# The transposed factor of a triangular inverse: transposes drained by ScalarE in place of a product and its sums

## The chip, the core and the metric

The kernel runs on one core of a Trainium2 chip. TensorE (PE) multiplies and transposes, VectorE (DVE) and ScalarE (ACT) do elementwise work and read PE's results from PSUM, GpSimd (POOL) splits the weights, and SyncE (SP) starts their loads. Each engine works through its own list of instructions in the order written and waits for the others by semaphores. The metric is device time in microseconds for one launch.

## The reference

The reference is one step of a two-layer decoder over a prompt of 1024 tokens and eight single-token samples. Layer 0 mixes tokens with a gated delta rule: projections to keys, queries, values and gates, a short convolution, then for each of 16 value heads a recurrence over chunks. Layer 1 is a diagonal state-space mixer; a SwiGLU layer follows each. What the change touches is the solve inside a chunk:

```
lmat = jnp.where(strict, jnp.einsum('nbhid,nbhjd->nbhij', kb, kc) * decay, 0.0)
sol = lax.linalg.triangular_solve(eye + lmat, rhs, left_side=True, lower=True, unit_diagonal=True)
```

The kernel does it with chunks of 128 tokens and by the inverse of the 128 x 128 unit triangular matrix.

## The kernel before, in words

The mix phase loops over 8 head groups `i` (one key head with its two value heads). In a group, dense steps project six weight tiles (L464), and then four quads `q` follow. A quad is two chunks times two heads, so four 128 x 128 matrices, held side by side in tiles of 512 columns.

The inverse of a quad is built in `levels` (L609). Y starts as the identity plus the mask of the innermost blocks, and TT_ holds its transpose, made once by four transposes (`first_t`, L506) and a ScalarE copy (L722). Then come six levels, each of which doubles the size of the blocks that are inverted. VectorE masks the matrix with the level's pattern into NM (L957). PE forms P = NM x TT_ (L620), which ScalarE copies to PP in two halves (L821), one half for each head. PE then forms PP x Y (PY, L634), which VectorE adds to Y (L1095). TT_ is brought up to date the same way: a third product (L630, called TP here), and two sums by VectorE (L1093). Level 6 has no TP, since its transpose isn't needed.

Each level has two slots in which other work is put, an even one ahead of P and an odd one between P and the products that use PP. The slots, numbered 0 to 11 in a quad, hold the recurrence over the quad before (`chain`: L517, L523, L529, L530, L536), the decays and the masked product for the next quad (L488, L498), transposes of values and keys (L588, L601), the samples' state (L575, L596), the output gate (L476), and pieces of the output projection of the group before (`out_piece`, L548; the first group has none). On ScalarE and VectorE the same slot numbers hold the halves of that work that belong to them, in their own lists: in slot 5 VectorE does the gate's products (L887, L888), and in slot 6 ScalarE waits for them and copies (L712).

The order is written out by hand in these lists. `p.after(engine, name)` makes an engine wait for a step; `use(b, engine, name)` claims PSUM bank b, waits until its former content has been drained, and notes who will drain this one. P and TP of a half share a bank: P in its first 256 columns, TP in the rest. PY has bank 2.

Of the kernel before, what the change touches and what calls it, by code (L numbers as in the profile page):

```python
# [19 lines left out]
ALU = mybir.AluOpType  # L20
AF = mybir.ActivationFunctionType

P = 128
D = 1024
KT = D // P
T = 1024
# [11 lines left out]
QCH = 2  # L38
# [14 lines left out]
def build(nc, dr, plan):  # L53
    ctx = ExitStack()
    with ctx:
        def sb(name, shape, dt=F32, c=ctx):
            return c.enter_context(nc.sbuf_tensor(name, shape, dt))
# [13 lines left out]
        ident = sb("ident", [P, P])  # L71
        gains = sb("gains", [P, 5, KT])
        ps = ctx.enter_context(nc.psum_tensor("ps", [P, 8, 512], F32))
# [235 lines left out]
        NM, PP, TT_, ATT_0, Y_1, VB, ATT_1, KD, EG, DEC_0, DEC_1, Y_0 = (dwork[:, i] for i in range(12))  # L309
# [101 lines left out]
        def f4(a_):  # L411
            return a_.rearrange("p a b -> p (a b)")

        def gate_cols(q):
            return slice(QCH * CH * q, QCH * CH * (q + 1)) if q < NQ else slice(T, N)
# [16 lines left out]
        def mix_pe(p):  # L432
# [4 lines left out]
            def use(b, who, name):  # L437
                if b in held:
                    p.after(*held[b])
                held[b] = (who, name)  # L440
                plan[("bank", p.pfx + name)] = b
                return b
# [166 lines left out]
            def levels(i, q):  # L609
                gq = f"{i}.{q}."  # L610
                Y = YY[q % 2]
                for l in range(1, 7):
                    slot(i, q, 2 * (l - 1))
                    p.after("DVE", gq + f"NM{l}")
                    for h in range(2):
                        p.after(*(("DVE", gq + f"T{l - 1}.{h}") if l > 1 else ("ACT", gq + "T0")))
                        b = use(h, "ACT", gq + f"P{l}.{h}")
                        for c in range(QCH):
                            j = 2 * h + c
                            ins = nc.tensor.matmul(ps[:, b, c * P:(c + 1) * P], NM[:, j], TT_[:, j], start=True, stop=True)  # L620
                        p.go(ins, gq + f"P{l}.{h}")
                    slot(i, q, 2 * (l - 1) + 1)
                    for h in range(2):
                        p.after("ACT", gq + f"P{l}.{h}")
                        p.after("DVE", gq + f"Y{l - 1}")
                        if l < 6:
                            b = use(h, "DVE", gq + f"T{l}.{h}")
                            for c in range(QCH):
                                j = 2 * h + c
                                ins = nc.tensor.matmul(ps[:, b, 256 + c * P:256 + (c + 1) * P], Y[:, j], PP[:, j], start=True, stop=True)  # L630
                            p.go(ins, gq + f"TP{l}.{h}")
                    b = use(2, "DVE", gq + f"Y{l}")
                    for j in range(4):
                        ins = nc.tensor.matmul(ps[:, b, j * P:(j + 1) * P], PP[:, j], Y[:, j], start=True, stop=True)  # L634
                    p.go(ins, gq + f"PY{l}")
# [39 lines left out]
        def mix_act(a):  # L675
            A = nc.scalar
# [26 lines left out]
            def gate_r(g, w):  # L703
                a.after("PE", g + "ones")
                a.do(A.activation(gate_buf(w), ps[:, a.bank(g + "oln"), 0:2 * w].rearrange("p (h n) -> p h n", h=2), AF.Ln, bias=eps_t[:, 0:1], scale=1.0 / P), g + "oln")
                a.go(A.activation(gate_buf(w), gate_buf(w), AF.Exp, scale=-0.5), g + "or")
# [68 lines left out]
            for i in range(HQK):  # L775
                g = f"{i}."
                e = i - 1
                if i:
                    gate_r(f"{e}.{NQ - 2}.", QCH * CH)
                    for k in (1, 2, 5, 6):  # L780
                        chain(e, NQ - 1, k)
                    gate_hi(f"{e}.{NQ - 2}.", gate_cols(NQ - 2), None)
                    state_out(e)
                evac(i, 0)
                if i:
                    gate_r(f"{e}.{NQ - 1}.", QCH * CH)
                evac(i, 1)
                if i:
                    gate_hi(f"{e}.{NQ - 1}.", gate_cols(NQ - 1), None)
                silu(i, 0)  # L790
                evac(i, 2)
                silu(i, 1)
                A.preload_act_table_set(LOGEXP)
                root(i, 0)
                decay(i, 0)
                evac(i, 3)
                root(i, 1)
                silu(i, 2)
                silu(i, 3)
                A.dma_start(dr["cso"][i], cso[:, :, :, :]).then_inc(out_conv, 16)  # L800
                A.dma_start(dr["cpo"][i], cpo[:, :, :]).then_inc(out_conv, 16)
                if i + 1 < HQK:
                    A.dma_start(cst[:, :, :, :], dr["cin"][i + 1]).then_inc(in_conv, 16)
                if i:
                    a.after("DVE", f"{e}.{NQ - 1}.og")
                for t in range(2):
                    for n in range(NC3):
                        a.after("PE", g + f"c{4 + t}.{n}")
                        a.go(A.activation(zb[:, t, blk(n)], ps[:, a.bank(g + f"z{t}.{n}"), 0:NB], AF.Silu), g + f"z{t}.{n}")
                        if t == 1 and n == 1:  # L810
                            first_t(i, 0)
                A.preload_act_table_set(LOGEXP)
                for q in range(NQ):
                    gq = f"{i}.{q}."
                    for l in range(1, 7):
                        slot(i, q, 2 * (l - 1))
                        for h in range(2):
                            a.after("PE", gq + f"P{l}.{h}")
                            if l > 1:
                                a.after("PE", gq + f"PY{l - 1}")  # L820
                            a.go(A.activation(f4(PP[:, 2 * h:2 * h + 2]), ps[:, h, 0:256], AF.Copy), gq + f"P{l}.{h}")  # L821
                        slot(i, q, 2 * (l - 1) + 1)
                    if q + 1 < NQ:
                        first_t(i, q + 1)
# [15 lines left out]
        def mix_dve(v):  # L840
            V = nc.vector
# [62 lines left out]
            def pairs(ap):  # L904
                return ap.rearrange("p (c n) -> p c n", n=P)
# [144 lines left out]
            for i in range(HQK):  # L1050
                g = f"{i}."
                e = i - 1
                if i:
                    chain(e, NQ - 1, 0)
                    scale_q(e, NQ - 1)
                    gate_sq(e, NQ - 2)
                    gate_mul(e, NQ - 2)
                    for k in (3, 4, 7):
                        chain(e, NQ - 1, k)
                tables(i)  # L1060
                if i:
                    gate_lo(e, NQ - 2)
                    gate_sq(e, NQ - 1)
                conv(i, 0)
                if i:
                    gate_mul(e, NQ - 1)
                    gate_lo(e, NQ - 1)
                squares(i, 0)
                conv(i, 1)
                squares(i, 1)  # L1070
                conv(i, 2)
                unit_norm(i, 0)
                decay(i, 0)
                conv(i, 3)
                unit_norm(i, 1)
                triangle(i, 0)
                first_y(i, 0)
                level_mask(i, 0, 1)
                for q in range(NQ):
                    gq = f"{i}.{q}."  # L1080
                    Y = YY[q % 2]
                    for l in range(1, 7):
                        slot(i, q, 2 * (l - 1))
                        if l < 6:
                            level_mask(i, q, l + 1)
                        elif q + 1 < NQ:
                            level_mask(i, q + 1, 1)
                        v.after("DVE", gq + f"Y{l - 1}")
                        for h in range(2):
                            hh = slice(2 * h, 2 * h + 2)  # L1090
                            if l < 6:
                                v.after("PE", gq + f"TP{l}.{h}")
                                v.go(V.tensor_tensor(TT_[:, hh], pairs(ps[:, h, 256:512]), TT_[:, hh], ALU.add), gq + f"T{l}.{h}")  # L1093
                        v.after("PE", gq + f"PY{l}")
                        v.go(V.tensor_tensor(Y, ps[:, 2, :].rearrange("p (j n) -> p j n", n=P), Y, ALU.add), gq + f"Y{l}")  # L1095
                        slot(i, q, 2 * (l - 1) + 1)
# [897 lines left out]
```

## Time and profile before

| | us |
|---|---|
| median of 3 runs | 3890.07 (3887.57 to 3891.27) |
| the profiled execution's own time | 3887.29 |
| its span | 3885.5 |
| PE busy in it | 3545.1 (91%) |
| VectorE busy | 2123.1 (55%) |
| ScalarE busy | 845.5 (22%) |

Busy time is summed over the instructions of an engine. PE stands for the matrix work and PEld for the loads of the stationary operand, which overlap it. The granted clock is the share of TensorE's full clock, 1.00 for 2.4 GHz and 0.50 for 1.2 GHz, as a mean over the stretch. The whole execution has 0.959. A program's fp32 product shows as two matrix instructions.

### The profile page before, as it was taken

The numbers are of one execution on the slowest core, as the hardware profiler recorded it, in microseconds if no ns is written. First come the engines' busy times: TensorE is split into PE (matmuls) and PEld (weight loads), VectorE is DVE, ScalarE is ACT, GpSimd is POOL, SyncE is SP. The second block draws the span as 40 slices with busy tenths as digits, with TensorE's granted clock in tenths as the row PEclk, the third lists the DMA queues.
The fourth block names the chain that finished last, engine by engine and source line by source line (L and its number), as shares of the span: only waits on it lengthen the run. The fifth ranks groups of instructions, "written<-read, shape, count | busy, mean of one in ns | idle before, by whom it ended". The sixth has DMA issues, their size and how long they took to land.

```text
span 3885.5 us, 56613 instructions
## 1 busy us (share of the span) xinstructions
PE 3545.1 (91%) x23849; PEld 3439.2 (89%) x23849; DVE 2123.1 (55%) x4331; ACT 845.5 (22%) x1691; POOL 836.9 (22%) x773
## 2 busy tenths in 40 slices
PE   4999999999999999997889999997679699999997
PEld 3989999998989898996879999996569699999997
DVE  3576757566666767575477577554632333333424
ACT  2333232423333332323100110111210210000001
POOL 1202020201111020201223232322323133323331
PEclk7999999999999999999989999999779899999998
DMA  2101010101001010100112222223831011111111
GB/s 78 34 23 36 28 41 17 41 23 40 29 30 40 23 36 28 35 17 29 33 40 75 71 70 77 71 77 110 231 90 49 22 44 49 44 50 49 45 49 55
DMA packets 91965, 197.29 MB, mean 51 GB/s; under 512 B 23232, under 2 KB 51008, under 8 KB 90560
## 3 DMA queue, kind: packets, MB, share of 16 engines
q1 hardware_dynamic: 65344, 152.42, 12.1%
q10 hardware_dynamic: 26368, 41.25, 3.2%
q8 instruction: 189, 3.10, 0.3%
q14 instruction: 64, 0.52, 0.0%
HBM read 152.69 MB, written 40.94 MB: 50 GB/s over the span
## 4 chain that ended last, share of the span: by engine, by line
PE 78%; DVE 17%; issue 2%; ACT 2%; DMA 1%; SPq 1%; POOL 0%; ACTq 0%; DVEq 0%; POOLq 0%
PE ps L210 25%; PE ps L464 14%; PE ps L1162 11%; PE ps L634 4%; PE ps L548 4%; PE ps L630 4%; PE ps L620 3%; PE ps L240 2%; PE ps L488 1%; DVE dwork L1095 1%; PE ps L523 1%; PE ps L536 1%; DVE hlo L269 1%; DVE S L987 1%; PE ps L476 1%
## 5 line engine op out<-in xcount | busy, mean ns | idle before, releaser
L210 PE MATMUL ps<-hhi,whi 128*128 128x344 f32 x2520 | 811.5, 322 | 87.2 <-DVE hlo L269 72.2
L210 PE MATMUL ps<-hhi,wlo 128*128 128x344 f32 x2520 | 808.8, 321 | 0.0
L210 PE MATMUL ps<-hlo,whi 128*128 128x344 f32 x2520 | 807.9, 321 | 0.0
L1843 POOL TENSOR_TENSOR wtick<-wtick 128x1 f32<-128x1 f32 x213 | 43.0, 202 | 2846.8 <-PE ps L210 977.6
L210 PEld LDWEIGHTS ps<-hhi,whi 128*128 128x128 f32 x2520 | 477.4, 189 | 90.5 <-issue 66.2
L1846 POOL TENSOR_TENSOR wlo<-wraw,whi 128x1024 fp32r<-128x1024 f32 x213 | 527.5, 2477 | 17.1
L210 PEld LDWEIGHTS ps<-hhi,wlo 128*128 128x128 f32 x2520 | 476.8, 189 | 0.0
L210 PEld LDWEIGHTS ps<-hlo,whi 128*128 128x128 f32 x2520 | 476.5, 189 | 0.0
L1215 DVE TENSOR_TENSOR ab<-ps,sg 128x344 f32<-128x344 f32 x132 | 68.2, 516 | 639.5 <-PE ps L210 628.1
L464 PE MATMUL ps<-hhi,whi 128*128 128x344 f32 x1152 | 386.2, 335 | 4.4 <-DVE dwork L847 1.9
L1162 PE MATMUL ps<-ahi,whi 128*128 128x344 f32 x1056 | 342.7, 325 | 32.3 <-DVE ab L1215 29.9
L464 PE MATMUL ps<-hhi,wlo 128*128 128x344 f32 x1152 | 371.7, 323 | 0.0
L464 PE MATMUL ps<-hlo,whi 128*128 128x344 f32 x1152 | 370.8, 322 | 0.0
L1162 PE MATMUL ps<-ahi,wlo 128*128 128x344 f32 x1056 | 340.8, 323 | 0.0
L1162 PE MATMUL ps<-alo,whi 128*128 128x344 f32 x1056 | 340.2, 322 | 0.0
L1230 DVE TENSOR_TENSOR x<-ps,x 128x344 f32<-128x344 f32 x528 | 257.8, 511 | 149.8 <-PE ps L1162 149.8
L1162 PEld LDWEIGHTS ps<-ahi,whi 128*128 128x128 f32 x1056 | 200.8, 190 | 37.9 <-DVE ab L1215 33.3
L464 PEld LDWEIGHTS ps<-hhi,whi 128*128 128x128 f32 x1152 | 219.5, 191 | 9.6 <-issue 8.8
L821 ACT ACTIVATE dwork<-ps 128x256 f32<-128x256 f32 x384 | 144.5, 383 | 362.7 <-PE ps L620 352.1
L464 PEld LDWEIGHTS ps<-hlo,whi 128*128 128x128 f32 x1152 | 219.2, 190 | 4.2 <-issue 3.4
L1844 POOL CAST whi<-wraw 128x1024 fp32r<-128x1024 f32 x213 | 221.5, 1040 | 0.0
L464 PEld LDWEIGHTS ps<-hhi,wlo 128*128 128x128 f32 x1152 | 219.4, 190 | 0.0
(328 smaller groups left out, 6092.2 us busy)
## 6 DMA issues: line engine op xcount, KB each, us to landing
wraw<-in_w SPq DMA_DIRECT2D x213, 512.0 KB, 3.3
tab<-keep_tab SPq DMA_DIRECT2D x8, 1088.0 KB, 6.4
S<-in_sin ACTq DMA_DIRECT2D x16, 512.0 KB, 3.5
out_sout<-S ACTq DMA_DIRECT2D x16, 512.0 KB, 2.6
keep_u<-hs SPq DMA_DIRECT2D x8, 580.0 KB, 3.0
uu<-keep_u SPq DMA_DIRECT2D x8, 580.0 KB, 7.9
keep_tab<-cp ACTq DMA_DIRECT2D x8, 576.0 KB, 6.1
keep_y<-yg SPq DMA_DIRECT2D x64, 68.5 KB, 2.3
```

What stands on the lines that cost most here:

```text
L210: ins = nc.tensor.matmul(out, w, r[:, kt, blk(n)], start=k == 0, stop=k == 3 * KT - 1)
L240: ins = nc.tensor.matmul(ps[:, banks + n, 0:NB], ones[:, :], nsq[:, kt % 2, blk(n)], start=kt == 0, stop=kt == KT - 1)
L464: ins = nc.tensor.matmul(ps[:, b, 0:NB], w, r[:, kt, blk(n)], start=k == 0, stop=k == 3 * KT - 1)
L548: ins = nc.tensor.matmul(ps[:, b, 0:NB], w[:, s, c:c + P], r[:, kt, blk(n)], start=k == 0, stop=k == 5)
L620: ins = nc.tensor.matmul(ps[:, b, c * P:(c + 1) * P], NM[:, j], TT_[:, j], start=True, stop=True)
L630: ins = nc.tensor.matmul(ps[:, b, 256 + c * P:256 + (c + 1) * P], Y[:, j], PP[:, j], start=True, stop=True)
L634: ins = nc.tensor.matmul(ps[:, b, j * P:(j + 1) * P], PP[:, j], Y[:, j], start=True, stop=True)
L821: a.go(A.activation(f4(PP[:, 2 * h:2 * h + 2]), ps[:, h, 0:256], AF.Copy), gq + f"P{l}.{h}")
L1162: ins = nc.tensor.matmul(out, w[:, s, c:c + P], r[:, e % 2, kt, blk(n)], start=q == 0, stop=q == 5)
L1230: v.go(V.tensor_tensor(x[:, m, blk(n)], ps[:, v.bank(f"x{e}.{m}.{n}"), 0:NB], x[:, m, blk(n)], ALU.add), f"x{e}.{m}.{n}")
L1844: G.tensor_copy(whi[:, slot, :], wraw[:, slot, :]).then_inc(w_hi, 1)
L1846: G.tensor_tensor(wlo[:, slot, :], wraw[:, slot, :], whi[:, slot, :].bitcast(F32), ALU.subtract).then_inc(w_split, 1)
```

## The change

TP and its two sums are gone. In their place, at levels 2 to 6 and after the even slot, PE waits for Y of the level before, transposes its four matrices (two for each half, into the columns where TP was), and ScalarE copies each half into TT_. P waits for that copy. ScalarE has the new copies behind what its even slot holds and ahead of the two copies of P.

```
                 for l in range(1, 7):
                     slot(i, q, 2 * (l - 1))
+                    if l > 1:
+                        p.after("DVE", gq + f"Y{l - 1}")
+                        for h in range(2):
+                            b = use(h, "ACT", gq + f"T{l - 1}.{h}")
+                            for c in range(QCH):
+                                ins = nc.tensor.transpose(ps[:, b, 256 + c * P:256 + (c + 1) * P], Y[:, 2 * h + c], ident[:, :])
+                            p.go(ins, gq + f"Tt{l - 1}.{h}")
                     p.after("DVE", gq + f"NM{l}")
                     for h in range(2):
-                        p.after(*(("DVE", gq + f"T{l - 1}.{h}") if l > 1 else ("ACT", gq + "T0")))
+                        p.after("ACT", gq + (f"T{l - 1}.{h}" if l > 1 else "T0"))
                         b = use(h, "ACT", gq + f"P{l}.{h}")
...
                     for h in range(2):
                         p.after("ACT", gq + f"P{l}.{h}")
                         p.after("DVE", gq + f"Y{l - 1}")
-                        if l < 6:
-                            b = use(h, "DVE", gq + f"T{l}.{h}")
-                            for c in range(QCH):
-                                j = 2 * h + c
-                                ins = nc.tensor.matmul(ps[:, b, 256 + c * P:256 + (c + 1) * P], Y[:, j], PP[:, j], start=True, stop=True)
-                            p.go(ins, gq + f"TP{l}.{h}")
                     b = use(2, "DVE", gq + f"Y{l}")
```

On ScalarE:

```
                         slot(i, q, 2 * (l - 1))
+                        if l > 1:
+                            for h in range(2):
+                                a.after("PE", gq + f"Tt{l - 1}.{h}")
+                                a.go(A.activation(f4(TT_[:, 2 * h:2 * h + 2]), ps[:, h, 256:512], AF.Copy), gq + f"T{l - 1}.{h}")
                         for h in range(2):
                             a.after("PE", gq + f"P{l}.{h}")
```

On VectorE:

```
                         v.after("DVE", gq + f"Y{l - 1}")
-                        for h in range(2):
-                            hh = slice(2 * h, 2 * h + 2)
-                            if l < 6:
-                                v.after("PE", gq + f"TP{l}.{h}")
-                                v.go(V.tensor_tensor(TT_[:, hh], pairs(ps[:, h, 256:512]), TT_[:, hh], ALU.add), gq + f"T{l}.{h}")
                         v.after("PE", gq + f"PY{l}")
```

## Rows read from the trace of the kernel before

**Rows 1.** The windows view over the eight groups: us, busy (count) by engine, clock, DMA.

```profile
166.00:1786.00 1620.00, 1536.76 (x11396) 1490.74 (x11395) 1085.64 (x2379) 530.63 (x1136) 211.39 (x171) 0.99 0.09 31
```

**Rows 2.** Waits of PE, 166 to 1785 us: total us, times, longest.

```profile
PE ps L596 <- DVE S L987: 18.9, 7, 2.7
PE ps L523 <- DVE dwork L968: 18.8, 20, 1.5
PE ps L476 <- DVE gsq L881: 16.6, 9, 2.2
PE ps L601 <- DVE S L987: 6.4, 7, 0.9
...
PE ps L529 <- DVE dwork L942: 4.4, 7, 0.6
```

**Rows 3.** Timeline, group 0, quad 3, level 6: start, us, engine, instruction [idle before].

```profile
272.70 0.97 PEld L634 LDWEIGHTS ps<-dwork 128*128 128x128 f32 x8
...
273.59 0.47 PEld L588 LDWEIGHTS ps<-ident,qkv 128*128 128x128 f32 x4
273.70 0.60 PE L588 MATMUL ps<-ident,qkv 128*128 128x128 f32 x4
273.90 0.69 DVE L1095 TENSOR_TENSOR dwork<-ps,dwork 128x512 f32<-128x512 f32 x1 [0.47 <-PE ps L634]
274.03 0.97 PEld L620 LDWEIGHTS ps<-dwork 128*128 128x128 f32 x8
...
274.34 0.60 ACT L763 ACTIVATE dwork<-ps 128x512 f32<-128x512 f32 x1 [1.52 <-PE ps L588]
...
274.83 0.78 ACT L821 ACTIVATE dwork<-ps 128x256 f32<-128x256 f32 x2
274.92 0.25 PEld L601 LDWEIGHTS ps<-ident,qkv 128*128 128x128 f32 x2
275.03 0.38 PE L601 MATMUL ps<-ident,qkv 128*128 128x128 f32 x2
275.73 0.97 PEld L634 LDWEIGHTS ps<-dwork 128*128 128x128 f32 x8 [0.55 <-ACT dwork L821]
```

**Rows 4.** Single lines, their instructions: duration in ns, minimum, median and maximum.

```profile
L630 PE MATMUL ps<-dwork x1280: 270/275/377, 169.1 to 1776.0; 128*128 128x128 f32 x183
...
L588 PE MATMUL ps<-ident,qkv x128: 272/273/273, 187.6 to 1777.4; 128*128 128x128 f32 x128
...
L821 ACT ACTIVATE dwork<-ps x384: 365/384/387, 168.7 to 1778.6; 128x256 f32<-128x256 f32 x192
...
L1093 DVE TENSOR_TENSOR dwork<-ps,dwork x320: 406/424/426, 170.0 to 1776.6; 128x256 f32<-128x256 f32 x160
```

**Rows 5.** Timeline, group 3, quad 1, level 3, whose odd slot is empty.

```profile
835.87 1.02 PEld L620 LDWEIGHTS ps<-dwork 128*128 128x128 f32 x8
...
836.67 0.83 ACT L821 ACTIVATE dwork<-ps 128x256 f32<-128x256 f32 x2 [5.08 <-PE ps L620]
...
837.11 0.97 PEld L630 LDWEIGHTS ps<-dwork 128*128 128x128 f32 x8 [0.22 <-ACT dwork L821]
```

**Rows 6.** Timeline, group 2, quad 3, level 4.

```profile
690.50 0.69 DVE L1095 TENSOR_TENSOR dwork<-ps,dwork 128x512 f32<-128x512 f32 x1 [0.47 <-PE ps L634]
...
691.53 1.02 PEld L620 LDWEIGHTS ps<-dwork 128*128 128x128 f32 x8
...
693.03 0.63 ACT L712 ACTIVATE ohi<-qkv 128x512 fp32r<-128x512 f32 x1 [4.51 <-DVE qkv L888]
...
693.69 0.52 PEld L523 LDWEIGHTS ps<-dwork 128*128 128x128 f32 x4 [1.15 <-DVE dwork L968]
```

**Rows 7.** Windows view: quad 0 of groups 4 and 3, and around one wait of L476.

```profile
1003.90:1037.80 33.90, 31.19 (x259) 30.84 (x258) 24.84 (x57) 8.12 (x17) 3.07 (x2) 1.00 0.05 16
...
789.30:824.60 35.30, 32.59 (x257) 32.36 (x256) 24.81 (x57) 8.06 (x17) 3.03 (x2) 0.95 0.05 16
...
708.00:714.00 6.00, 4.63 (x17) 4.15 (x18) 2.75 (x6) 1.32 (x2) 0.00 (x0) 0.72 0.00 0
```

## The prediction

> **What bounds the kernel now.** I read the windows view first. From 166 to 1786 us, where the eight head groups run (projections and the levels of the triangular inverse), PE is busy 1536.8 of 1620 us at a granted clock of 0.99, VectorE 1085.6 and ScalarE 530.6 [rows 1]. PE is the bound there; the change touches nothing outside it. What PE idles is in the waits view: almost all of it ends on a VectorE instruction of the quads (L968, L987, L881, L942), and the sums of L1093 are not among them [rows 2]. So the question for each edit is what it does to PE's own sequence: work taken out, and new waits put in. VectorE's relief as such is worth nothing.
>
> One level on PE is now: an even slot of filler, P (L620), an odd slot, TP (L630), PY (L634). In the timeline of a level without a wait each of these groups of four products takes 0.89 us of PE's issue time (PY at 272.70, the next group at 273.59) [rows 3]. The two new inputs of the next P, T's halves, are summed by VectorE while PE does PY, so P never waits for them.
>
> **The change, part by part.** There are 5 exchanges in a quad, 4 quads in a group, 8 groups: 160, and 20 in a group.
>
> *The product TP goes, transposes come.* L630 has 1280 records for the 640 products the code issues, so a product is two passes; L588 has 128 for 128 transposes, one pass [rows 4]. Four transposes take 0.44 us (L588 at 273.59, L620 at 274.03) [rows 3]. Saved: 0.89 - 0.44 = 0.45 us each, 9.0 us a group, 72 us in all. The 320 sums of 0.42 us (L1093) leave VectorE and 320 copies of 0.38 us (L821's form) go to ScalarE [rows 4]: neither is the bound, 0 by themselves.
>
> *Wait B, between the transposes and P.* Nothing stands between them in PE's order, so PE waits out a whole drain. Worked from [rows 3]: two transposes (L601) start at 274.92 and leave the array at 275.03 + 0.38 = 275.41, 0.49 later; ScalarE starts 0.04 after the last transpose (L588 ends 274.30, L763 starts 274.34); a half takes 0.38 [rows 4]; from its end to PE's next load 0.06 (L821's first half ends 837.05, L630 loads at 837.11, [rows 5]) to 0.12 (275.61 to 275.73, the end of L821 and the load of L634). Sum 0.97 to 1.03 from the first transpose. PE's queue is free 0.44 after it: B = 0.56 us. The second half follows 0.38 behind the first while P's first half occupies 0.45, no more wait. 18 of the 20 exchanges: 10.1 us.
>
> *The other two* are level 4 of quads 2 and 3. There ScalarE's queue holds, ahead of the T copies, the gate's copy L712, which waits for L887 and L888 on VectorE. Y is done at 690.50 + 0.69 = 691.19, L712 at 693.03 + 0.63 = 693.66 [rows 6]. Now P starts at 691.53 without caring. Then: T's first half at 694.04, P at 694.1, 2.9 after Y; the transposes are off PE's queue 0.79 after Y (filler up to 691.53, then 0.44). Wait 2.13, two a group: 4.3 us. Behind P stands today's wait of L523 for L968 (load at 693.69, P issued by 692.42): 1.25 us, which is over before P is; it is given back, -2.5 a group.
>
> *Wait A, before the transposes.* They need Y, which PE used to need only a P and an odd slot later. Y ends 1.00 after PY is off the queue (273.59; 273.90 + 0.69) [rows 3]; with 0.06 to PE that is 1.06. Filler of the even slots, counted in the code: 0.89 to 0.90 in nine exchanges of a group (an out_piece, or the four products of a chain step or of drow), wait 0.16 each; 0.44 in two (level 6 of quads 1 and 3, the vT transposes), 0.62 each; 1.3 or more in nine, none. 2.7 us, and 0.3 for level 2 of quad 0, where the mask (L957) holds Y back by more than TP used to hide: 3.0 a group.
>
> *PY now waits for both halves of PP.* TP began after the first: PE loads it 1.24 after P (835.87 to 837.11), while the second half ends at 837.50, 1.63 after P [rows 5]. Only where the odd slot is short is it seen: 0.48 in quad 1 level 3, 0.35 in quad 2 level 1, 0.22 in quad 3 level 3. 1.1 us a group.
>
> *Given back elsewhere.* At level 6, kT and the transposes for T0 wait for VectorE (L601 for L987, 6.4 us in 7 times [rows 2], and some 0.6 for L936 in quad 1). P comes 1.0 to 1.6 later after Y5 than now, so both go: 0.9 + 0.6. In quad 3, L529's 0.6 [rows 2] turns into a wait for Y, which comes 0.85 (two sums) sooner: I take 0.4. The long wait of L596 (2.7 us, 7 times) hangs on Y5 and stays. -1.9 a group.
>
> Sum for a group: -9.0 + 10.1 + 4.3 - 2.5 + 3.0 + 1.1 - 1.9 = +5.1 us; seven groups 36 us. The first group has no out_pieces: six even slots lose their 0.9 of cover (5.4) and short odd slots add about 1: 11.5 us. Together +47 us.
>
> *The clock.* The waits of L476 come to 16.6 us in 9 times and those of L596 to 18.9 us in 7 [rows 2]. Where the clock fell, after L596's wait at 818.3, quad 0 of that group took 35.3 us at a mean of 0.95; the same quad of the next group, with the same wait and the clock at 1.00, took 33.9 [rows 7]. A fall to the lower level costs 1.4 us. Read window by window in the same way, it fell behind 6 of the 7 waits of L596, behind 4 of the 8 of L476 (one stands in [rows 7], 0.72 over six us), and behind none of the waits up to 1.5 us that L523 has. The 16 new waits of 2.13 us lie between the two kinds, nearer to L476's, at 0.5 to 0.6: 9 falls, 13 us. Bounds: 0 and 16 x 1.4 = 22 us.
>
> +60 us on the profiled run's own 3887.3 us (its span of 3885.5 and 1.8 around it) is 3947; the median of the runs shown lies 2.8 above it: **3950 us**.
>
> Against this change stands a rule of the Trainium skill, "TensorE: Matmul & The Clock Gate", Part 4 (PE-mode transpose): work in transpose mode does not count as PE being busy the way products do, so it does not hold the full clock. The trace allows it: the four L588 transposes stand right ahead of L596's wait, after which the clock fell more often than after L476's, which has none. By the rule each exchange's 0.44 us adds to the idle time beside it; by row it doesn't. It is the second rival.
>
> **Rivals.**
> 1. *The waits that VectorE causes absorb the new ones.* If P's later start also swallowed what is left of L523's 18.8 us and half of L476's 16.6 us, and B and A came out at their low ends (0.53, 0.10), the sum falls by 2 + 8 + 4 + 9, with no falls of the clock 13 more: 3914. Against: L476 hangs on work after the last level. 10%.
> 2. *The clock goes with the transposes.* Waits A and B and the transposes between them make 0.62 + 0.44 + 0.56 = 1.6 us in level 6 of quads 1 and 3, and 1.06 + 0.44 + 0.56 = 2.1 in six levels of the first group; if those 22 places and all 16 long ones drop the clock, it is 38 x 1.4 = 53 us in place of 13: 3990. For: the share of falls behind L596 against L476. Against: the transposes cut these waits in two, and today's waits up to 1.5 us had none behind them. 13%.
> 3. *Faster: the drain is hidden.* The mechanism is B alone. If P could start while ScalarE drains, as PY does behind PP's drains under an odd slot, 18 x 8 x 0.56 = 81 us go from the 60: 3869. It decides at B = 0.56 - 60/144 = 0.14 us: under that the change gains. A half's copy alone is 0.38, and PE's order holds nothing to put beside it, so 5%.
>
> **How the numbers follow.** Forecast 72%, rivals 10, 13 and 5%. The range, 3912 to 3995, spans rivals 1 and 2 and the bounds of A and B (0.05 us on 160 exchanges is 8 us each way) and leaves the third out. No change that a measurement of this kernel can tell is within 0.2%, 7.8 us: 3%, from a still larger rival 1. Faster 6%, slower 91%.
>
> **What would show it.** L630's records gone and 640 new single-pass ones in their place; PE's idle time in the levels up by 110 to 130 us (A, B and PY's wait, less what is given back), put down to ScalarE copies and L1095's sum, while PE's busy time falls by about 70; P's load 0.97 to 1.03 after the first transpose; a wait of 2.1 us in level 4 of quads 2 and 3, and none of L523's 1.0 there; mean clock of the stretch at 0.97 to 0.98 rather than 0.99. B under 0.3 us, or a level that was bound by VectorE after all (its wait for PY at L1095 gone from the trace), would make the prediction wrong.

## The result and the profile after

The kernel after takes 3932.61 us (median of 4 runs, 3929.4 to 3934.34) against 3888.82 us of the kernel before beside it: a ratio of 1.0114, 95% interval 1.0097 to 1.0132, 44 us slower. Forecast were 3950 us with a range of 3912 to 3995: right in its sign and in its range, 17 us too much in its size.

The profiled execution has 3934.23 us and a span of 3932.5. The eight groups now run from 166 to 1830 us instead of 1785 [rows 1]. What comes behind them takes nearly the same (PE busy 1897 us in the last 2102 us, 1898 in the last 2099 before): 45 of the 47 us between the two spans are lost in the levels. First the windows view of that stretch, then PE's waits in it (total us, times, longest). PE stands for the products, PEld for the loads of the stationary operand, and a PEld wait is what PE's queue stood still for.

```profile
166.00:1830.00 1664.00, 1522.17 (x10755) 1423.02 (x10755) 974.12 (x2059) 637.95 (x1456) 211.39 (x171) 0.98 0.10 30
```

```profile
PEld ps L627 <- ACT dwork L821: 101.4, 160, 1.9
PEld ps L619 <- DVE dwork L1095: 33.0, 77, 1.1
PEld ps L596 <- DVE S L992: 20.6, 7, 2.9
PEld ps L635 <- ACT dwork L826: 18.7, 34, 1.9
...
PEld ps L529 <- DVE dwork L947: 12.0, 7, 1.7
...
PEld ps L523 <- DVE dwork L973: 7.0, 17, 1.2
...
PEld ps L601 <- DVE S L992: 1.1, 7, 0.2
```

In the kernel after, L619 are the transposes, L821 the copies of T, L627 is P, L826 the copies of P, L635 PY. The top row is wait B: P waits for the T copy in all 160 places, 101 us. The second is wait A, the fourth PY's wait. The same view of before, for four rows that the change shortened or lengthened:

```profile
PEld ps L523 <- DVE dwork L968: 26.7, 34, 1.7
...
PEld ps L601 <- DVE S L987: 7.8, 7, 1.1
...
PEld ps L506 <- DVE dwork L936: 6.4, 8, 0.8
...
PEld ps L529 <- DVE dwork L942: 5.8, 7, 0.8
```

L523's and L601's waits shrank as forecast (by 20 and 7 us). L506's, with 2.1 more us in another row, is gone: 8.5 us, where I had 5. L529's doubled where I had it shrink.

The timeline of group 3, quad 1, into level 4 shows one exchange (start, us, engine; a part of the longer rows is another level):

```profile
862.25 0.52 PEld L619 LDWEIGHTS ps<-ident,dwork 128*128 128x128 f32 x4
862.41 0.60 PE L619 MATMUL ps<-ident,dwork 128*128 128x128 f32 x4
862.83 0.66 ACT L821 ACTIVATE dwork<-ps 128x256 f32<-128x256 f32 x2 [2.29 <-PE ps L619]
863.26 0.86 PEld L627 LDWEIGHTS ps<-dwork 128*128 128x128 f32 x7 [0.49 <-ACT dwork L821]
```

P loads 1.01 us after the first transpose. From [rows 3] I had 0.97 to 1.03. Where the transposes themselves begin after a wait it is 0.91: there the first of them starts with its load, while here it starts 0.16 behind it (862.25 and 862.41); I had not made this difference. The other kind of wait, level 4 of quad 3 in the same group:

```profile
928.65 0.69 DVE L1095 TENSOR_TENSOR dwork<-ps,dwork 128x512 f32<-128x512 f32 x1 [1.00 <-PE ps L635]
...
929.70 0.52 PEld L619 LDWEIGHTS ps<-ident,dwork 128*128 128x128 f32 x4
...
931.18 0.63 ACT L713 ACTIVATE ohi<-qkv 128x512 fp32r<-128x512 f32 x1 [3.84 <-DVE qkv L893]
...
931.72 0.64 ACT L821 ACTIVATE dwork<-ps 128x256 f32<-128x256 f32 x2
932.13 0.97 PEld L627 LDWEIGHTS ps<-dwork 128*128 128x128 f32 x8 [1.92 <-ACT dwork L821]
...
933.02 0.53 PEld L523 LDWEIGHTS ps<-dwork 128*128 128x128 f32 x4
```

The gate's copy (L713, L712 of before) stands ahead of T's copies exactly as in [rows 6]; Y is done at 929.34, P loads 2.79 later, and L523 no longer waits. But the clock, which I had fall after such waits, stayed at 1.00 over this one. The windows view, around this wait and around one of L596's waits (the clock is the number before the last two):

```profile
929.00:935.00 6.00, 4.31 (x34) 4.06 (x33) 3.42 (x7) 2.95 (x9) 0.17 (x2) 1.00 0.00 0
1059.00:1065.00 6.00, 3.51 (x15) 3.11 (x16) 2.77 (x8) 1.13 (x3) 0.00 (x0) 0.72 0.00 0
```

I counted the falls of the clock in the stretch of the levels: 11 before, 15 after. Only 1 of the 16 waits of level 4 has one beside it; all 7 of L596's have.

### The profile page after: what moved, and what is told of

It reads as the page before. It is cut to its first block, busy times and chain, and to the rows that moved or that the text cites. A ratio compares the mean times of both kernels' runs of the same rounds, so it can differ in the third digit from the quotient of the medians.

```text
span 3932.5 us, 55272 instructions
## 1 busy us (share of the span) xinstructions
PE 3529.4 (90%) x23209; PEld 3371.0 (86%) x23209; DVE 2012.1 (51%) x4011; ACT 953.2 (24%) x2011; POOL 838.3 (21%) x773
## 4 chain that ended last, share of the span: by engine, by line
PE 76%; DVE 16%; ACT 3%; issue 2%; DMA 2%; SPq 0%; POOL 0%; DVEq 0%; ACTq 0%; POOLq 0%
PE ps L210 24%; PE ps L464 14%; PE ps L1162 11%; PE ps L627 5%; PE ps L635 4%; PE ps L548 4%; PE ps L240 2%; ACT dwork L821 2%; PE ps L488 1%; PE ps L619 1%; DVE dwork L1095 1%; PE ps L596 1%; PE ps L529 1%; PE ps L476 1%; DVE n_r L1371 1%
## 5 line engine op out<-in xcount | busy, mean ns | idle before, releaser
L210 PEld LDWEIGHTS ps<-hhi,whi 128*128 128x128 f32 x2520 | 477.6, 190 | 90.3 <-issue 66.0
L210 PEld LDWEIGHTS ps<-hhi,wlo 128*128 128x128 f32 x2520 | 477.2, 189 | 0.0
L210 PEld LDWEIGHTS ps<-hlo,whi 128*128 128x128 f32 x2520 | 476.7, 189 | 0.0
L464 PE MATMUL ps<-hhi,whi 128*128 128x344 f32 x1152 | 386.1, 335 | 4.4 <-DVE dwork L852 1.9
L464 PE MATMUL ps<-hhi,wlo 128*128 128x344 f32 x1152 | 370.3, 321 | 0.0
L464 PE MATMUL ps<-hlo,whi 128*128 128x344 f32 x1152 | 369.7, 321 | 0.0
L627 PE MATMUL ps<-dwork 128*128 128x128 f32 x1536 | 224.7, 290 | 61.9 <-ACT dwork L821 61.5
L627 PEld LDWEIGHTS ps<-dwork 128*128 128x128 f32 x1536 | 192.4, 195 | 101.4 <-ACT dwork L821 101.4
L1095 DVE TENSOR_TENSOR dwork<-ps,dwork 128x512 f32<-128x512 f32 x192 | 132.6, 691 | 270.5 <-PE ps L635 270.5
L962 DVE TENSOR_TENSOR dwork<-dwork,lev 128x512 f32<-128x512 f32 x192 | 144.5, 753 | 195.6 <-PE ps L627 193.9
L1181 ACT ACTIVATE sg<-ps 128x344 f32<-128x344 f32 x132 | 59.3, 457 | 706.3 <-PE ps L210 706.3
```

What stands on the lines that cost most here:

```text
L210: ins = nc.tensor.matmul(out, w, r[:, kt, blk(n)], start=k == 0, stop=k == 3 * KT - 1)
L464: ins = nc.tensor.matmul(ps[:, b, 0:NB], w, r[:, kt, blk(n)], start=k == 0, stop=k == 3 * KT - 1)
L962: v.go(V.tensor_tensor(NM, DEC[q % 2], lev[:, 1 + l].unsqueeze(1).to_broadcast([P, 4, P]), ALU.mult), g + f"NM{l}")
```

## The experiments

Each is an edit on the kernel before or after, or on an earlier one of them. The first four ran beside the kernel before at 3886.7 us, the next four at 3887.15, the last two at 3890.3.

**e1_bare: the product alone.** On before; TP and its sums taken out, nothing put in. The transpose stays that of level 1.

```
-                        if l < 6:
-                            b = use(h, "DVE", gq + f"T{l}.{h}")
...
-                            p.go(ins, gq + f"TP{l}.{h}")
```

> The kernel before without TP and its two sums, and with nothing in their place; TT_ keeps the transpose that it has at level 1, so the inverse is left incomplete. This prices the product alone. By my terms: 160 x 0.89 = 143 us less, and 9 more because PY then waits for both halves of PP; the waits that VectorE causes stay: 3755 to 3770 us. If instead the levels were held by VectorE's or ScalarE's chain (P, copy, PY, sum), the product would be mostly hidden: 3830 or more.

Measured 3763.75 us, ratio 0.9684 (0.967 to 0.9699), 123 us less. TP was on the path nearly in full. Quad by quad the trace gives 3.97 and 4.1 us less in quads 1 and 2, of 5 x 0.89 = 4.45; and 3.07 in quad 3, where L529's wait grows to the 12 us that the kernel after has too. So this wait is not the transposes' doing: without TP, PE comes to it 0.9 us sooner.

**e2_both: PY's wait alone.** On before.

```
-                    for h in range(2):
-                        p.after("ACT", gq + f"P{l}.{h}")
+                    p.after("ACT", gq + f"P{l}.1")
+                    for h in range(2):
```

> The kernel before, but PE waits for both halves of PP ahead of TP. This prices the term of PY's wait by itself. By my terms it costs 1.05 us in each group and about 1 more in the first: 9 us, 3898. If the wait is covered by the odd slots everywhere: 3889, no change.

Measured 3888.29 us, ratio 1.0009 (1.0 to 1.0018): 3.5 us by the ratio, and by its interval anything from nothing to 7, so under the 9 that I expected. The trace has it. The places are the forecast ones: quad 1 level 3 +0.45, quad 2 level 1 +0.29, quad 3 level 3 +0.15, and 0.16 comes back at the level behind the first. 0.73 us a group instead of 1.05. This trace has 7 falls of the clock in the levels where before has 11, though the edit adds no work: so a difference of four falls between two traces need not come from an edit.

**e3_noB: wait B taken away.** On after; the copies are made, into a tile that nothing reads, and P works on the first transpose.

```
-                        p.after("ACT", gq + (f"T{l - 1}.{h}" if l > 1 else "T0"))
+                        p.after("ACT", gq + "T0")
...
-                            b = use(h, "ACT", gq + f"T{l - 1}.{h}")
+                            b = use(2, "ACT", gq + f"T{l - 1}.1") if h == 0 else 2
...
-                                a.go(A.activation(f4(TT_[:, 2 * h:2 * h + 2]), ps[:, h, 256:512], AF.Copy), gq + f"T{l - 1}.{h}")
+                                a.go(A.activation(tsink[:, :], ps[:, 2, 256 * h:256 * h + 256], AF.Copy), gq + f"T{l - 1}.{h}")
```

> The kernel after, with the same transposes and the same number and width of ScalarE copies, but from PY's bank into a tile that nothing reads (bf16), and with P not waiting for them; P works on the first transpose, so the inverse is left incomplete. This takes wait B alone away. The trace of after shows B at about 0.5 us in 18 places of a group and 2.0 in two, of which some 0.8 comes back as L523's wait: 8 x (18 x 0.5 + 2 x 1.2) = 91 us less, some 5 given back at level 6: 3840 to 3855. The rival, that the loss is the clock (transposes that don't hold it): B gone and the time still near 3920, with as many falls of the clock.

Measured 3839.24 us, ratio 0.9878 (0.9865 to 0.9892): 93 us less than after. Against it, 0.45 to 0.52 us went in the ordinary places (medians over groups 1 to 7) and 1.1 to 1.2 net in each long one: P comes 1.9 sooner there, and some 0.8 returns as L523's wait. The trace has 9 falls of the clock for the 15 of after, which at 1.4 us each is 8 of the 93. This settles the cause of the loss: with the product's 0.45 us saved and B not paid, the kernel is 1.2% under the one before.

**e4_prod and e8_twice: passes, and transposes and the clock.** A pass here is one matrix instruction of the profile. On after; each transpose as a plain product with the identity, and each transpose done twice in transpose mode.

```
-                                ins = nc.tensor.transpose(ps[:, b, 256 + c * P:256 + (c + 1) * P], Y[:, 2 * h + c], ident[:, :])
+                                ins = nc.tensor.matmul(ps[:, b, 256 + c * P:256 + (c + 1) * P], Y[:, 2 * h + c], ident[:, :], start=True, stop=True)
```

```
+                                for _ in range(2):
+                                    ins = nc.tensor.transpose(ps[:, b, 256 + c * P:256 + (c + 1) * P], Y[:, 2 * h + c], ident[:, :])
```

> The kernel after, with each transpose done as a plain product with the identity, which gives the same numbers. If a plain product is two passes and a transpose one, PE works 160 x 0.45 = 72 us more, of which the wait for the first half's copy hides about 0.2 us each: +35 to +50, 3970 to 3985. By the Trainium skill's rule that transposes don't count as PE being busy, the clock should fall less often than the 15 times of the kernel after and some of it comes back, 10 us at most. If the passes don't matter: 3933.

> The kernel after, with each of the 640 transposes issued twice into the same columns. PE's order and the time of each group are those of e4_prod (two passes for each), only in transpose mode. So 0.27 us more for an exchange where nothing else waits, 39 us by my terms: 3970, less what the clock does. e4_prod came to 3955 with 5 falls of the clock in these stages against 15 of the kernel after. If transposes hold the clock as products do: 3955 and few falls. By the Trainium skill's rule that they don't: 15 falls or more, and 3965 to 3975.

Measured 3954.93 us (ratio 1.018, 1.0165 to 1.0196) and 3952.15 us (1.0169, 1.0155 to 1.0183): +22 and +20 us over after (26 and 21 by the ratios). The first is under my 35 to 50; the second is near the 3955 us that I gave it if transposes hold the clock as products do. The two are alike in PE's work, as their traces say:

```profile
L619 PEld LDWEIGHTS ps<-ident,dwork x1280: 186/192/333, 170.2 to 1843.0; 128*128 128x128 f32 x183
```

```profile
L620 PEld LDWEIGHTS ps<-ident,dwork x1280: 137/140/230, 170.5 to 1842.3; 128*128 128x128 f32 x183
```

The first is e4_prod, 1280 records for 640 products, the second e8_twice, 1280 for 1280 transposes; after has 640. So the step's saving rests on passes, one against two. An exchange costs 0.27 us more in e4_prod and 0.22 in e8_twice, not 0.45, since wait B shrinks (PEld waits for the T copy some 54 and 62 us, in after 101). That makes 35 to 43 us; the traces have 6 and 8 falls of the clock where after has 15 (I had first stopped counting at 1830 us, ahead of e4_prod's sixth at 1849), which would give some of it back at 1.4 us each (13 and 10 us). The Trainium skill's rule ("TensorE: Matmul & The Clock Gate", Part 4) is not borne out here: 640 more passes in transpose mode went with fewer falls, not more, and with the time of the products. Five of after's falls stand beside no wait of L476 or L596; of these e4_prod and e8_twice have only the first, at 170 us. But before and e2_both differ by four falls as well, and that twice the work fills PE and so holds the clock would fit both; one trace of each can't show it.

**e5_gate: the long waits.** On after.

```
-                if s == 6 and q >= 2:
+                if s == 7 and q >= 2:
                     gate_hi(f"{i}.{q - 2}.", gate_cols(q - 2), f"{i - 1}.out{KT - 1}.{q - 2}" if i else None)
```

> The kernel after, with ScalarE's copy of the gate (L713 of after) in slot 7, behind the copies of T and P of level 4, instead of slot 6 ahead of them. If the 2.0 us waits of level 4 in quads 2 and 3 are this copy's doing, they go down to 0.5, and L523 waits some 0.25 for VectorE: 16 x 1.25 = 20 us less, 3913. If they came from VectorE's own queue (the gate's products), nothing changes: 3933. If VectorE then stands at the gate's subtraction, it is slower than 3933.

Measured 3910.37 us, ratio 1.0065 (1.0047 to 1.0083): 22 us less than after (19 by the ratios), level 4 of quads 2 and 3 shorter by 1.18 each, and nothing else moved in the other quads. PE's longest wait for a T copy falls from 1.7 us to 0.3:

```profile
PE ps L627 <- ACT dwork L821: 61.5, 151, 1.7
```

```profile
PE ps L627 <- ACT dwork L821: 38.5, 151, 0.3
```

(The first is after, the second e5_gate.) One copy, placed where it cost nothing before, was nearly half of the loss. With the long waits gone the trace still has 14 falls of the clock for the 15 of after, so hardly any of them came from those waits.

**e6_split and e7_both: work behind the transposes.** On after; each slot can be called in parts, and the part that ScalarE doesn't drain comes between the transposes and P. e7_both has e5_gate's edit too.

```
+                        slot(i, q, 2 * l - 3, 1)
+                        slot(i, q, 2 * (l - 1), 1)
                     p.after("DVE", gq + f"NM{l}")
...
+                    slot(i, q, 2 * (l - 1), 2)
                     slot(i, q, 2 * (l - 1) + 1)
...
+                late = s in (6, 9)
+                if q and s in CHAIN_SLOT and part == late:
...
+                if piece and i and part == (s in (3, 7, 9) or s == 2 and q > 0):
```

> The kernel after, with work that ScalarE doesn't drain put between the transposes and P: the out_pieces of slots 3, 7 and 9 and of slot 2, the gate's sums, the chain's kS of slot 6 and its last product of slot 9; and the second drow of quad 0 behind P of level 6. Nothing is left out. By my terms wait B goes in about 15 of 20 places, 0.3 to 0.5 us each, some 2 us at level 6 of quad 0 where P passes L596's wait, and PY's wait takes 0.8 back in quad 3: 8 to 9 us a group, 60 to 67 us, 3866 to 3873, faster than the kernel before. If the waits only move (Y or PP late instead): 3915 or more.

> e6_split and e5_gate in one. Of the 20 us of e5_gate 15 are left, since the chain's kS already covers part of it and L523's wait for L968's sums grows to about 0.65: 3852 to 3858. The rival, that VectorE is the bound once PE's waits are gone: no gain over e6_split.

Measured 3878.68 us (ratio 0.9981, 0.9972 to 0.999) and 3854.48 us (0.9914, 0.99 to 0.9928). Both are faster than the kernel before, and e7_both is where I expected it. e6_split gained 52 us on after by the ratios, 8 short of its 60 to 67: quads 0 to 2 are 5.1, 2.2 and 1.7 us shorter than in after, but quad 3 is 1.05 longer. The timeline of e7_both in group 3, quad 3, level 5 has the reason (POOL is GpSimd; L966 is the mask, L1099 Y's sum, L620 the transposes):

```profile
901.40 2.38 POOL L1850 TENSOR_TENSOR wlo<-wraw,whi 128x1024 fp32r<-128x1024 f32 x1
...
901.59 2.73 DVE L966 TENSOR_TENSOR dwork<-dwork,lev 128x512 f32<-128x512 f32 x1
...
904.25 0.68 DVE L1099 TENSOR_TENSOR dwork<-ps,dwork 128x512 f32<-128x512 f32 x1
904.98 0.42 PEld L620 LDWEIGHTS ps<-ident,dwork 128*128 128x128 f32 x4 [2.10 <-DVE dwork L1099]
```

The mask takes 2.73 us instead of 0.69 while GpSimd subtracts; the sum of Y stands behind it, and now the transposes wait for Y. The moved out_piece is the last reader of its weights and starts that split.

Part of the gain in quad 0 is not wait B at all: L596's wait, 20.6 us in both before and after, is gone from the list, since the second drow now stands behind P of level 6.

**e9_keep7 and e10_late0: where the split falls.** On e7_both, then on e9_keep7.

```
-                if piece and i and part == (s in (3, 7, 9) or s == 2 and q > 0):
+                if piece and i and part == (s in (3, 9) or s == 7 and q < 3 or s == 2 and q > 0):
```

```
-        PIECE_SLOTS = (... (0, 3, 4, 6, 7), (0, 3, 4, 6, 7))
+        PIECE_SLOTS = (... (0, 3, 4, 6, 7), (1, 3, 4, 6, 7))
```

> e7_both, but in quad 3 the out_piece of slot 7 stays in its odd slot. In e7_both that piece is the last to use its weights and sits ahead of P of level 5; GpSimd starts to split the next weights behind it, and VectorE's mask for level 6 (L966) takes 2.7 us instead of 0.7 at its side, which makes Y and with it the transposes 2 us late. If that is the cause, the mask is back at 0.7, and of the 2 us a group some 0.5 is given back as wait B and PY's wait is 0.4 better: 7 x 2 = 12 to 15 us less than e7_both's 3854, 3840. If L966's length has nothing to do with the piece: 3854 to 3858.

> e9_keep7, and the first out_piece of quad 3, after which the other weights' half is free, moved from slot 0 to slot 1. L529's wait of 1.5 us in each of 7 groups stands behind a gate product (L942 of before) that takes 2.57 us beside GpSimd's split. By the same cause the split now starts some 1.5 us later, on instructions of VectorE that nobody waits for at once: up to 7 x 1.5 = 10 us less, 3830. If it then falls on the mask of level 3 or the scaling of keys, the wait only moves: 3840 or a few us more.

e9_keep7: 3859.63 us, ratio 0.9917 (0.9904 to 0.9931), no better than e7_both's 0.9914. Its trace has the mask of quad 3 at its normal length, PE's waits for Y at 26.9 us in place of 36.5 and quad 3 0.84 us shorter. But its profiled run is 3844.86 us while the other five lie at 3858 to 3862; their mean granted clock is 0.955 to 0.958 against 0.962. Of the runs of before beside e7_both, the two at 0.957 took 3891.5 and 3892.9 us and the two at 0.962 3879.5 and 3887.2, so the clock may well be most of the 15 us. The mechanism is seen in a trace, worth 6 us in seven groups where I had 12 to 15, and the gain is not measured. e10_late0: 3838.67 us, ratio 0.9868 (0.9854 to 0.9882), 19 us less than e9_keep7 by the ratios. But the two profiled runs are only 5.4 us apart (3844.86 and 3839.47), so how much of the 19 is the edit and how much e9_keep7's clock isn't shown. What the trace shows is near the 10 that I gave it: L529's wait is gone from its list, PE's wait at L523 grows from 7.8 to 15.1 us, and quad 3, from one quad's end to the next, is 1.6 us shorter, 11 us in seven groups; the row of e9_keep7 that went (L951 is L942 of before):

```profile
PE ps L529 <- DVE dwork L951: 10.6, 7, 1.5
```

It is the fastest of the kernels that build the whole inverse, 1.3% under the kernel before, with the transposes in it. Whether it is the transposes that win is not shown: no run gives the kernel before the same order. Two of the moves need no transposes, and the waits that they take away, 20.6 us at L596 and 5.8 at L529, are in before too: together as much as half of the 51 us.

## Why the prediction was right, and where it was not

*The sum.* By quad, in groups 1 to 7 (median of P of level 1 to PY of level 6, after less before) the trace has +1.8, +1.1, +0.1 and +2.0: 4.9 us a group against 5.1 forecast, and +14.2 in the first group against 11.5. That is 48.5 us for the quads, but it holds six more falls of the clock than before, some 8 us at 1.4 each: about 40 us without the clock where I had 47. Between the groups there are two falls less (-3), and so the stretch grew by 45.

*The saving, 0.45 us.* Right: two passes against one (e4_prod, e8_twice), and TP wholly on the path (e1_bare).

*Wait B.* 101 us measured as PE's queue saw it, 115 forecast (8 x 14.4), the term of the sum that was most too large. e3_noB gives 93 us for it net of what comes back. 0.49 in most of the ordinary places for my 0.56, 1.9 in the long ones for my 2.13.

*Waits A and PY's.* 33 us for A against 29 (8 x 3.0 and the first group's bare slots, 5.4); PY's wait 18.7 us where PE already waited 7.7 for PP before (L630 and L634), 11 more for my 9 to 10. By itself it is less, 0.73 a group (e2_both).

*Given back.* L523 -20 us and L601 -7 as forecast, L506 -8.5 for my 5. L536's 2.9 us went too, which I had not counted. The 0.4 at L529 was wrong: TP's going brings PE to it sooner and it costs 6 us more instead, which e1_bare shows without any transposes.

*The clock, +13 us.* This is the step that failed. I put the new 2 us waits between L476's and L596's by their length and gave them 9 falls; 1 of 16 had one, and e5_gate, without these waits, has 14 falls for 15. I had also compared unlike measures: my 2.13 was a stand of PE's queue, and by that measure L476's waits are 2.16 and L596's 2.94, so the new ones did not lie between the two. The count went from 11 to 15, 6 us at 1.4 each: three new ones in the first group, where bare slots bring waits A and B together, two in level 3 of quad 0, where PE has only its 0.5 us waits, one more at L596, and two fewer at L476 and at a wait of L464 between the groups. What sets the long waits of level 4 apart from L476's, which have falls at nearly the same length, I don't know: PE's own idle time beside them is 1.7 us against 1.97, and the work around them is as dense.

*The 17 us.* The profiled runs lie 46.9 us apart (3934.2 and 3887.3) and I had 60: 13 us too much, of which the clock term is 7 and the rest of the sum 6. I then added 2.8 us for the median of before over its profiled run; after has its median 1.6 under it.

*The readout of PE's busy column* was also off. I had busy time fall by 70 us and idle time rise by 110 to 130. Busy fell by 15 (1536.76 to 1522.17) and idle rose by 59. The column counts a group's last matmul to the end of its flight, 1.06 us for a group that holds the queue 0.89; that these ends lie over the next group in a dense stream and are added ahead of a wait would explain it, but I have not worked it out. The PEld waits are the measure that fits the sum: all of them together rose from 119 to 227 us. These 107, less the 72 saved, and 6 for the clock are 41 of the 45 us.

*The rivals.* None came true. The drain is not hidden (rival 3): B is at 0.5, and the point where the change would gain was 0.14. L476's waits still come to 16.0 us for 16.6, so rival 1's large term was absent. Rival 2 had 38 places drop the clock; of its six bare levels of the first group two have a fall beside them, of its 16 long waits one, of level 6 of quads 1 and 3 none.

## What to carry to other kernels

An operation that is cheaper for an engine can lose if it moves a drain into that engine's own order. Half the passes saved 0.45 us and the drain between transposes and product cost 0.5: price the round trip through the draining engine first, then look for work to put beside it. Before adding a step to an in-order queue, read what already stands in it ahead of that place and what that waits for; here one copy made a 0.5 us wait of 1.9. And a kernel that lost by a trade may be brought back by its order: with filler behind the transposes and three more moves it is 1.3% under the kernel that had the product. Before the trade itself is given the credit, the old kernel has to get the same order, which was not run here.

## What the runs showed that I had not expected

A VectorE instruction with both inputs in SBUF takes 2.45 to 2.73 us instead of 0.42 or 0.69 when it meets GpSimd's subtraction of 2.4 us, and ends 0.3 to 0.6 us after it. It happens in the same two places of all seven groups (L962 and L947 in after), because both are tied to the order of PE's work. The Trainium skill says so ("SBUF — State Buffer", Who interferes with whom): such an instruction takes turns with a GpSimd instruction that reads SBUF, and the later one is held up in full. The traces agree, and e10_late0's shows what the meeting is worth where PE waits behind it: the 1.6 us of quad 3.

A wait of PE of 1.7 us is passed at the full clock 15 times in 16, while of the eight of 1.97 to 2.2 us at L476 four had a fall beside them before the change and three after it, and of the seven of 2.7 us at L596 six and seven.
